# First modulation turned by products with ones, the first products taken feature by feature, and the down products in the order 5 1 3 2 4 7 6

## The reference, cut to what matters

```python
mod = c_act @ ada_w[l] + ada_b[l]
sh1, sc1, g1, sh2, sc2, g2 = jnp.split(mod, N_MOD, axis=-1)
h = modulate(rms_norm(x, norm_attn_g[l]), sh1, sc1)      # h * (1 + scale) + shift
x = x + g1[:, None, :] * hybrid_mixer(h, ...)            # begins with h @ w_in
h = modulate(rms_norm(x, norm_ffn_g[l]), sh2, sc2)
x = x + g2[:, None, :] * swiglu(h, w_gate[l], w_up[l], w_down[l])
return rms_norm(x, final_norm_g)
```

## Time and profile before

| | |
|---|---|
| median of 3 runs | 1424.18 us (1422.64 to 1425.14) |
| profiled execution: its own time | 1420.86 us |
| profiled execution: its span | 1419.1 us |
| PE busy | 1347.4 us, 95% of the span |
| DVE busy | 999.2 us, 70% |
| POOL busy | 810.1 us, 57% |
| ACT busy | 689.8 us, 49% |
| granted TensorE clock, mean | 0.982 of full speed |

### The profile page before, as it was taken

One profiled execution on the slowest core, in us unless ns is written; L12 is line 12 of the kernel. 1 busy time (PEld: TensorE's weight loads), 2 busy tenths in 40 slices (PEclk: granted clock), 3 DMA queues, 4 the chain that ended last, 5 costly groups with the idle time before them and its releaser, 6 DMA issues.

```text
span 1419.1 us, 20205 instructions
## 1 busy us (share of the span) xinstructions
PE 1347.4 (95%) x7003; PEld 1149.9 (81%) x7003; DVE 999.2 (70%) x1600; ACT 689.8 (49%) x1368; POOL 810.1 (57%) x537
## 2 busy tenths in 40 slices
PE   1899999999999999999999899999999999999987
PEld 0888788888799999898887688888888888788775
DVE  4743779999785888986556855555566666478697
ACT  4623346563467677765335443444433333455535
POOL 3141402323436433580007998889998885799775
PEclk9799999999999999999999999999999999999999
DMA  9122322353423866432311233333323334997963
GB/s 379 59 68 68 93 71 75 100 155 105 125 72 106 261 197 196 140 99 90 122 47 40 75 104 104 112 112 111 112 89 105 112 118 142 383 379 253 315 216 144
DMA packets 126286, 200.59 MB, mean 141 GB/s; under 512 B 10637, under 2 KB 60997, under 8 KB 125162
## 3 DMA queue, kind: packets, MB, share of 16 engines
q1 hardware_dynamic: 126186, 199.30, 42.5%
HBM read 156.99 MB, written 42.27 MB: 140 GB/s over the span
## 4 chain that ended last, share of the span: by engine, by line
PE 77%; DVE 10%; POOL 4%; issue 3%; DMA 2%; ACT 1%; SPq 1%; ACTq 0%; DVEq 0%; POOLq 0%
PE PS L2014 19%; PE PS L2016 19%; PE PS L2015 19%; PE PS L2192 8%; PE PS L2156 4%; PE PS L2175 3%; POOL rawb L951 2%; POOL BS L958 2%; DVE AS L1885 1%; PE PS L2177 1%; PE PS L2180 1%; DVE acc L1378 1%; DMA rawb<-in_w_down_dram 1%; DVE PS L1937 1%; DMA rawa<-gu_scratch 1%
## 5 line engine op out<-in xcount | busy, mean ns | idle before, releaser
L939 POOL TENSOR_TENSOR WS<-WSf,WS 128x512 fp32r<-128x512 f32 x110 | 171.1, 1563 | 0.7 <-ACT WS L1197 0.7
L1197 ACT CAST WS<-WSf 128x512 fp32r<-128x512 f32 x110 | 68.4, 622 | 206.5 <-POOL WSf L929 205.6
L929 POOL TENSOR_TENSOR WSf<-rawg 128x512 f32<-128x512 f32 x55 | 76.1, 1384 | 144.2 <-PE PS L2016 143.3
L2192 PE MATMUL PS<-Vn,PT 128*128 128x64 f32 x1152 | 143.4, 270 | 0.0
L2014 PE MATMUL PS<-yh,WS 128*128 128x512 f32 x352 | 137.9, 392 | 2.9 <-DVE yl L1805 2.9
L2192 PEld LDWEIGHTS PS<-Vn,PT 128*128 128x128 f32 x1152 | 139.7, 193 | 0.6
L2015 PE MATMUL PS<-yl,WS 128*128 128x512 f32 x352 | 137.7, 391 | 0.0
L2016 PE MATMUL PS<-yh,WS 128*128 128x512 f32 x352 | 137.5, 391 | 0.0
L2014 PE MATMUL PS<-BS,AS 128*128 128x512 f32 x308 | 121.5, 395 | 6.3 <-DVE x1s L1969 4.1
L2015 PE MATMUL PS<-BS,AS 128*128 128x512 f32 x308 | 120.8, 392 | 0.0
L2016 PE MATMUL PS<-BS,AS 128*128 128x512 f32 x308 | 120.7, 392 | 0.0
(11 more groups left out here) (322 smaller groups left out, 3707.9 us busy)
## 6 DMA issues: line engine op xcount, KB each, us to landing
rawb<-in_w_down_dram SPq DMA_DIRECT2D x132, 256.0 KB, 4.8
rawa<-gu_scratch SPq DMA_DIRECT2D x77, 256.0 KB, 5.0
gu_scratch<-GS SPq DMA_DIRECT2D x55, 256.0 KB, 4.6
raw<-in_w_in_dram SPq DMA_DIRECT2D x24, 512.0 KB, 3.9
rawg<-in_w_gate_dram SPq DMA_DIRECT2D x22, 512.0 KB, 4.3
rawu<-in_w_up_dram SPq DMA_DIRECT2D x22, 512.0 KB, 4.4
ada<-in_ada_w_dram SPq DMA_DIRECT2D x8, 1024.0 KB, 9.8
qk_scratch<-stage SPq DMA_DIRECT2D x32, 256.0 KB, 2.1
```

The lines of the kernel that those rows point to most:

```text
L929: pool.tensor_tensor(WSf[m % N_SLOT][:], left(i, mat, a), left(i, mat, b), ALU.add if sign > 0 else ALU.subtract).then_inc(ws_sum, 1)
L939: pool.tensor_tensor(lo, WSf[m % N_SLOT][:] if b else left(i, mat, a), hi.bitcast(F32), ALU.subtract).then_inc(ws_ready, 1)
L2192: last = pe.matmul(PS[:, 6 + hd % 2, t * DH:(t + 1) * DH], PT[:, u % 2, j * P:(j + 1) * P], Vn[(hd // 4) % 2][:, j, cols], start=j == 0, s ...
```

## The change: what it does

Front:
1. The order of loads: tiles 4 to 7 of `x` stand ahead of pieces 4 to 7 of `ada1`, and the four weight pieces of the first chunk behind them.
2. ACT divides both halves of `x` by their roots, ahead of the rounding of the weight pieces; the fourth piece is rounded after the first four turned blocks. DVE only takes the reciprocals.
3. The last step of `acc1` is made in two parts, the scale's columns first. PE then sums over the partitions itself: sixteen matmuls with a column of ones, one result column each, scale first. DVE reads those 8 columns directly; the two sums along rows are gone.
4. PE takes the first four row tiles feature by feature: it turns one k, and multiplies another k for tiles 0 to 3 (`front`). Tiles 4 and 5 come together, k by k, then tiles 6 and 7 as before.
5. POOL's split of the second chunk's weights waits in addition for the last remainder `hl` (`nt_lo`).

Down stage:
6. `DOWN` is 5 1 3 2 4 7 6. "2" is now only subtracted from 22, `partial_result` follows in the steps of the fifth product, and quadrant 21 is finished with "4", whose results DVE takes up during the sixth.

```diff
-    order = [("tile", 0, t) for t in range(TT)]
-    order.insert(TT // 2 + 2, ("angles",))
-    order.insert(3, ("second half", 1))
-    order.insert(2, ("second half", 0))
+    order = [("front",), ("angles",)] + [("tile", 0, t) for t in range(TT // 2 + 2, TT)]
...
-DOWN = ["5", "1", "3", "4", "2", "7", "6"]
+DOWN = ["5", "1", "3", "2", "4", "7", "6"]
...
+            for t in range(TT // 2, TT):
+                load_x(t)
+            for k in range(KT // 2, KT):
+                load_ada(k)
             for n in range(PIECES):
                 load_piece(n)
-            for k in range(KT // 2, KT):
-                load_ada(k)
-            for t in range(TT // 2, TT):
-                load_x(t)
...
                 if ch == 1 and n % PIECES == 0:
                     pool.wait_ge(nt_pe, 2 * KT)
+                    pool.wait_ge(nt_lo, 2 * KT)
...
+            first_norm(0)
+            first_scaled(0)
             first_norm(1)
+            first_scaled(1)
+            for n in range(PIECES - 1):
+                first_rounded(n)
             act.wait_ge(mod1_ok, 2)
-            first_turned(0, 0)
-            first_turned(0, 1)
+            first_turned(0, 0, KT // 2)
+            first_rounded(PIECES - 1)
+            first_turned(0, KT // 2, KT)
+            first_turned(1, 0, KT // 2)
...
+            def front():
+
+                evac_tile(0, 0)
+                first_turned(1, 4, 5)
+                evac_tile(0, 1)
+                first_turned(1, 5, KT)
+                for t in range(2, TT // 2 + 2):
+                    evac_tile(0, t)
...
-                dve.scalar_tensor_tensor(out=acc1[:], in0=ada1[:, k, :], scalar=cact[:, k:k + 1], in1=acc1[:],
-                                         op0=ALU.mult, op1=ALU.add).then_inc(acc1_ok, 1)
+                for cols in (slice(D, 2 * D), slice(0, D)) if k == KT - 1 else (slice(0, 2 * D),):
+                    dve.scalar_tensor_tensor(out=acc1[:, cols], in0=ada1[:, k, cols], scalar=cact[:, k:k + 1],
+                                             in1=acc1[:, cols], op0=ALU.mult, op1=ALU.add).then_inc(acc1_ok, 1)
...
-                elif form == "4":
-                    last = down_add("11", p, tt, ALU.add)
                 elif form == "2":
                     chained(down_add("22", p, tt, ALU.subtract))
-                    chained(down_result("21", p, tt))
                     return
+                elif form == "4":
+                    chained(down_add("11", p, tt, ALU.add))
+                    last = down_result("21", p, tt)
...
-                    elif p == 4:
+                    elif p == 3:
                         partial_result(p, j // 2)
...
-            turn_x(0, 0)
-            pe.wait_ge(acc1_ok, KT)
-            for part in range(2):
-                for j in range(part * KT, (part + 1) * KT):
-                    last = pe.transpose(PS[:, j // 4, (j % 4) * P:(j % 4 + 1) * P], acc1[:, j * P:(j + 1) * P], ident[:])
+            turn_x(0, 0, KT // 2)
+            for i, part in enumerate((1, 0)):
+                pe.wait_ge(acc1_ok, KT + i)
+                for k in range(KT):
+                    j = part * KT + k
+                    last = pe.matmul(PS[:, part, k:k + 1], acc1[:, j * P:(j + 1) * P], ones[:, 0:1], start=True, stop=True)
                 last.then_inc(mod1_pe, 1)
-            turn_x(0, 1)
...
+            def front():
+                for k in range(KT - 2):
+                    if k < KT // 2:
+                        turn_x(0, KT // 2 + k, KT // 2 + k + 1)
+                    else:
+                        turn_x(1, k - KT // 2, k - KT // 2 + 1)
+                    for t in range(TT // 2):
+                        tile(0, t, rows_of=range(k, k + 1))
+                turn_x(1, 2, 4)
+                for t in range(TT // 2):
+                    tile(0, t, rows_of=range(KT - 2, KT))
+                    turn_x(1, KT // 2 + t, KT // 2 + t + 1)
+                for k in range(KT):
+                    for t in range(TT // 2, TT // 2 + 2):
+                        tile(0, t, rows_of=range(k, k + 1))
```

More of the change, by code:

```diff
@@ L996, in first_norm, with first_turned @@
                 act.activation(stat[:, 1, cols], stat[:, 0, cols], ACT.Sqrt, bias=epsc[:], scale=1.0 / D).then_inc(root_ok, 1)
-            def first_turned(half, part):
-                for k in range(part * KT // 2, (part + 1) * KT // 2):
+            def first_turned(half, first, stop):
+                for k in range(first, stop):
                     g = half * KT + k
@@ L1012, in _, with first_scaled, first_rounded @@
             act.wait_ge(const_st, 5)
[L1013 to L1017, removed]
+            def first_scaled(half):
+                act.wait_ge(rstd_ok, half + 1)
+                for t in range(half * TT // 2, (half + 1) * TT // 2):
+                    act.activation(xs[:, t, :], xs[:, t, :], ACT.Identity, scale=rstd[:, 0, t:t + 1]).then_inc(xn_ok, 1)
+            def first_rounded(n):
                 act.wait_ge(raw0_in[n], 32)
                 act.copy(wsl(n)[0][:, 0:2 * IDXW], raw0[:, n, 0:2 * IDXW]).then_inc(w_hi, 1)
+            first_norm(0)
+            first_scaled(0)
             first_norm(1)
+            first_scaled(1)
+            for n in range(PIECES - 1):
+                first_rounded(n)
             act.wait_ge(mod1_ok, 2)
-            first_turned(0, 0)
-            first_turned(0, 1)
+            first_turned(0, 0, KT // 2)
+            first_rounded(PIECES - 1)
+            first_turned(0, KT // 2, KT)
+            first_turned(1, 0, KT // 2)
             def evac_tile(ch, t):
@@ L1078, in forget @@
                 act.wait_ge(cumT_ok, 2)
+            def front():
[5 more added lines that the diff above has]
+                    evac_tile(0, t)
             for step in PROJ_ORDER:
-                if step[0] == "tile":
+                if step[0] == "front":
+                    front()
+                elif step[0] == "tile":
                     if step[3:] != (0,):
@@ L1093, in _ @@
                     forget()
-                elif step[0] == "second half":
-                    first_turned(1, step[1])
                 elif step[0] == "angles":
@@ L1337, in over_rms @@
                 dve.reciprocal(rstd[:, 0, cols], stat[:, 1, cols]).then_inc(rstd_ok, 1)
[L1339 to L1343, removed]
-                    dve.tensor_scalar(xs[:, t, :], xs[:, t, :], rstd[:, 0, t:t + 1], None, ALU.mult).then_inc(xn_ok, 1)
             def first_lo(half):
@@ L2016, in three, with turn_x @@
                 return pe.matmul(dst, left[1], right[0], start=False, stop=last)
-            def turn_x(half, part):
-                for k in range(part * KT // 2, (part + 1) * KT // 2):
+            def turn_x(half, first, stop):
+                for k in range(first, stop):
                     g = half * KT + k
@@ L2119, in _ @@
                     cumulative()
-                elif step[0] == "second half":
-                    turn_x(1, step[1])
                 elif step[0] == "angles":
```

33 lines of the change are left out of this document (16 added, 17 removed).

## The result

The changed kernel took 1416.12 us, the median of 20 runs (1406.42 to 1425.17), beside 1424.26 us for the kernel before (20 runs, 1420.02 to 1430.11). The ratio is 0.9943, with a 95% interval of 0.9926 to 0.996: 8.1 us less, where 14.0 were forecast.

The account below looks back on a forecast made before the run. PE was taken as the bound, busy 1347.4 of 1419.1 us, with time lost in waits and at the lower clock. Front 5.9 plus down stage 8.1 gave 14.0 us off 1424.18: 1410 us forecast, range 1406 to 1416.

Parts of the forecast that it names:

- the added wait on POOL: Front, POOL's splits for the second chunk: waiting for the last `hl` costs nothing, with 2 us of cover.
- the last sum: Front, last step of `acc1` on DVE, in halves: scale's half done at 36.0 us, shift's at 37.2.
- The second chunk: Front: its first product on PE starts at 80.15 us, 5.9 us ahead of 86.05.
- The products with ones: Front, PE's sums over partitions: eight take some 2.0 us at the half clock, the pace of transposes.
- wrong if ACT's first turned block starts after 41: Front, a sign against the forecast: ACT was to begin its turned blocks at 40.3 us instead of 43.09.
- What the front saves, the end saves: Whole kernel: behind the second chunk's first product PE works on without a pause the change touches; 5.9 us.
- 8.1 us: Down stage, total gain from the new product order: 6.6 + 1.5 us.
- 1.5 us for the wait in the fifth product: Down stage: PE's wait for the late "3" results goes, 1.5 us gained.
- that one stall costs 6.6 us: Down stage near 1375 us: PE's 4.1 us wait costs 6.6 us with the low clock, all gained.
- a window between 1290 and 1380 still shows PE under 10 us in 10: Down stage, a sign against the forecast, which expected no wait of PE for `x1s` there.
- this leaves 23.7 ... DVE is done 4.5 us early: Down stage: DVE takes up "4" in 23.7 us (32.5 less 8.8), where PE gives 28.2 us.
- the down stall moves: Rival, down stage: POOL falls behind in three summed products, DVE with it; new wait costs some 4.5 us, 1414.5; 13 in 100.

Follow-up runs that it names:

- e0: The changed kernel run once more, nothing altered; 0.9945 of the kernel before.
- e5: The changed kernel with sixteen transposes and DVE's two sums in place of the products with ones, scale first; 0.9952 of the kernel before.
- e2: The changed kernel with the old order of the down products, so the front's changes alone; 0.9955 of the kernel before.
- e4: The changed kernel with four remainders `BS` of the last two down products (steps 62, 65, 70, 73) on POOL instead of DVE; 0.9917 of the kernel before.
- e9: The same kernel as e4, run once more; 0.9932 of the kernel before.
- e8: The changed kernel with the old down order and four remainders `BS` (steps 56, 59, 62, 65) on POOL instead of DVE; 0.9951 of the kernel before.
- e6: The changed kernel with four more remainders `BS` of the last two down products (steps 61, 64, 69, 72) on DVE; 0.9938 of the kernel before.
- e3: The changed kernel without POOL's added wait for the last remainders `hl`; 0.9956 of the kernel before, 1417.81 us.

## Why the prediction was right and wrong

**The direction was right, and most of the front's mechanism.** PE doesn't wait for `hl`, nor in between, nor for the weights; the added wait on POOL costs nothing; the last sum came at 35.98 where 37.2 was forecast, 0.9 us of it because the first loads were earlier in this execution. The second chunk began at 80.31 for 80.15. That hit is made of two errors. *The products with ones* were taken as 2.0 us for each eight "at the pace of transposes", with the row at 599 us as support; they took 3.5. I had divided that row by the wrong number of products. With it the mark "wrong if ACT's first turned block starts after 41" was met: 42.07. The forecast had 2.8 us to gain up to that point, and only 1.0 came, 0.9 of it from the earlier loads. The first product came at 44.1 instead of 42.3. Against it, from there to the second chunk 36.2 us passed, and not 37.85: the clock was full some 3.6 us after the first product started, not 4.5, and by subtraction the transposes between products cost less than the 2.05 us that I had put on them. The clock's part of this differs between executions of the same kernel: in e0 it was full 2.0 us after the first product (45.8 against 43.77; 16 matmuls started from 46 to 48 there, 11 in after), and in e5, whose products are the same, only some 5 us after (0.60 of full speed from 48 to 50).

**"What the front saves, the end saves"** agrees with the totals, not with the pair of traces. The front saved 4.7 us of the forecast's 5.9, and e2, with the front alone, is 6.4 us faster (3.7 to 9.3). But in the one pair of traces that I could look at the middle was 7.4 us longer after than before. The profile of before was a short one in the middle. The forecast added the 3.3 us by which before's median lies above its traced execution; for a difference of medians that is fair.

**The step that failed is the down stage's: "8.1 us", which came out as 3.3.** Its smaller term, 1.5 us for the wait in the fifth product, was right and came as 1.8. Its larger term, "that one stall costs 6.6 us", was right as the price of the stall and wrong as a gain: the seventh product became 1.3 us shorter on the mean, not 6.6. The 4.1 us wait is gone, but DVE is now late there itself (1.2 us for `x1s`, which also meets the mark "a window between 1290 and 1380 still shows PE under 10 us in 10") and later again for `BS` (3.1 us). Only with four remainders off DVE did the seventh product lose 6.3 us (e4, e9). Wrong was "this leaves 23.7 ... DVE is done 4.5 us early". DVE began with the results of "4" at 1349.21, 7.7 us behind the end of that product on PE (1341.47). In before it began with those of "2" 5.0 us behind (1343.15, 1348.16), so it was 2.7 us late at the start. From there it took 25.5 us, where before took 31.1 and the forecast took 8.8 off: 3.2 us more than 22.3. Together that is the way from 4.5 us early to 1.2 late. It has two reasons.

- *DVE's durations were taken from before as if they belonged to the operation.* They depend on what POOL does beside it, and on how DVE's own operations lie to POOL's. Over the down stage `AS` took 1115 ns on the mean before, 1111 in e2 and 1159 in e8; in the ten traces of the new order it took 1316 to 1366. For seventy-five of them that is 100.3 us in after against 83.0 before. DVE was idle for a quarter of the stage before (165.5 us busy of 219.7); now it is busy for 187.0 of 216.2.
- *DVE was summed up for one product at a time and not through the last three.* The last product's last four steps are taken row tile by row tile (`LATE_DOWN = 4`), so PE needs every remainder four steps ahead of the end. With the old order PE never waits there, though it has by then stopped for 4.1 us at 1375, which gave DVE that much time. With "4", "7" and "6" in a row and no such stop DVE had no lead left. PE stopped behind the matmul of 1391.69 for the last `BS`, 3.1 us, and then the clock fell: 16 matmuls started in 8.30 us, with a mean clock of 0.79.

The rival "the down stall moves" (13 in 100, 1414.5) had this mechanism nearly, POOL behind and DVE with it. It put POOL first; but POOL had room (2.0 and 2.1 us of waiting for its data at 1373 and 1381), and e4 gave it four more remainders and gained. The rival's 4.5 us for the new wait with its clock stands beside 4.8 us that went missing; that the two are so near is luck, as its waits were to be POOL's. Forecast 14.0 less 1.2 in the front and less 4.8 in the down stage is 8.0, by the means of the traces.

**The contention.** Here are DVE's rows of after at 1383 us (start, us), and then POOL's:

```profile
1379.77 0.68 DVE L1899 TENSOR_TENSOR BS<-rawb,BS 128x512 fp32r<-128x512 f32 x1
...
1381.57 0.69 DVE L1945 TENSOR_TENSOR PS<-PS,CD 128x512 f32<-128x512 f32 x1
1382.29 0.70 DVE L1946 TENSOR_TENSOR PS<-PS,g2r 128x512 f32<-128x512 f32 x1
1383.03 0.69 DVE L1947 TENSOR_TENSOR x1s<-PS,x1s 128x512 f32<-128x512 f32 x1
1383.63 1.71 DVE L1894 TENSOR_TENSOR AS<-rawa,AS 128x512 fp32r<-128x512 f32 x1
1385.26 1.78 DVE L1899 TENSOR_TENSOR BS<-rawb,BS 128x512 fp32r<-128x512 f32 x1
1386.97 1.77 DVE L1894 TENSOR_TENSOR AS<-rawa,AS 128x512 fp32r<-128x512 f32 x1
```

```profile
1383.50 1.29 POOL L949 TENSOR_TENSOR rawb<-rawb 128x512 f32<-128x512 f32 x1 [0.70 <-DMA rawb<-in_w_down_dram]
1384.76 1.74 POOL L956 TENSOR_TENSOR BS<-rawb,BS 128x512 fp32r<-128x512 f32 x1
```

Operations of one size: those that read PSUM (the memory that PE writes its results to) take 0.67 to 0.70 us wherever they stand, those with both inputs in SBUF 0.68 when POOL is still (the `BS` at 1379.77) and up to 1.82 beside it. The Trainium skill, SBUF — State Buffer, "SBUF: two separate sides", says that a DVE operation with two SBUF inputs and a GpSimd operation that reads SBUF take a shared pair of ports as a lock, the one that comes second waiting for the whole of the other's instruction. These rows agree: the `AS` that starts at 1383.63, just behind POOL's instruction of 1383.50, takes 1.71, which is 0.69 and most of that instruction's 1.29.

How full POOL is over the stage does not set the price alone. POOL is busy for 86% of it in after (185.6 us of 216.2) and in e8 (187.3 of 217.6), with 1355 ns and 1159 for `AS`; and for 82% before (179.7 of 219.7) and in e6 (179.1 of 217.7), with 1115 and 1316. What goes with the dear ones is that DVE itself hardly pauses (187.0 and 186.6 us busy in after and e6, 165.5 and 166.8 before and in e8). Its remainders then stand one right behind the other: 47 of 95 in after, 1.58 us on the mean, and 32 before, 1.33 us; those behind a pause take 1.08 and 1.05. Whether the lateness makes them dear or the price makes DVE late, no run here separates.

## What to carry to other kernels

A change of order that leaves every operation as it is still changes their durations, when two engines get in each other's way: the SBUF-only operations of DVE don't keep the price that they had, so put a range on it (here 0.7 to 1.8 us for each) where DVE and GpSimd both work without a pause, and sum a shared engine through to the last deadline, not stage by stage. Where both are full, shifting work from one to the other buys less than its length (9.0 us off, 3.3 back), and it can buy 5 us in one stretch (e4) and next to nothing in another (e8). A wait that is gone is not yet a gain, when the engine that was waited for has no time to spare at the next deadline. Count the instructions in a row before dividing by them, and take a second trace before reading a difference of 3 us from two.

The version to keep is the changed kernel with four remainders less on DVE (e4 and e9): 0.9917 and 0.9932 of before, where the change alone has 0.9943 and 0.9945. The step between them rests on the traces more than on the totals.

## What the runs showed of the hardware

- An fp32 matmul with one result column appears as two in the trace: 16 products with ones are 32 matmuls, 6.98 us at the lower clock, 0.22 us each, so one product costs 0.44 us there; a transpose of 128 x 128 takes 0.23 (3.67 us for sixteen in e5).
- Tiny operations of DVE also grow beside POOL's splits: the eight steps of 128 x 8 on the rope angles took 6.84 us in after (73.17 to 80.01), 0.86 each, and PE's work hid it. Before, when POOL was done at 79.34, the same eight took 1.95 us.
- The granted clock behind 370 us fell for anything from nothing (e3) to about 14 us (e0, after), in code that no run here changes; by the rows it makes the middle longer or shorter by up to 7 us (282.9 us in e3 and 289.9 in e0, from the first logits to the first output product). It stays open what decides it.
